# The last six d_ff blocks of a down projection as Strassen-Winograd periods, with two weight sums made by adding transfers

## The reference

```python
h = x + 0.5 * swiglu(rmsnorm(x, g_ffn1), w1g, w1u, w1d)      # FFN 1
u = rmsnorm(h, g_mix)
...                                                          # projections, rotary, two kinds of attention
h = h + concat([oa, ob]) @ w_out
h = h + 0.5 * swiglu(rmsnorm(h, g_ffn2), w2g, w2u, w2d)      # FFN 2
y = rmsnorm(h, final_norm)

def swiglu(x, wg, wu, wd):
    return (jax.nn.silu(x @ wg) * (x @ wu)) @ wd
```

## Time and profile before

| | us |
|---|---|
| median of 3 runs (1061.0 to 1065.07) | 1061.13 |
| the profiled execution's own time | 1062.71 |
| its span, first to last instruction | 1060.9 |
| TensorE busy in the span | 1039.9 (98%) |
| VectorE busy | 835.1 (79%) |
| ScalarE busy | 539.8 (51%) |
| GpSimd busy | 86.7 (8%) |
| mean granted TensorE clock | 0.994 of full speed |

### The profile page before, as it was taken

One profiled execution on the slowest core, in us unless ns is written; L12 is line 12 of the kernel. 1 busy time (PEld: TensorE's weight loads), 2 busy tenths in 40 slices (PEclk: granted clock), 3 DMA queues, 4 the chain that ended last, 5 costly groups with the idle time before them and its releaser, 6 DMA issues. The chain is left out here.

```text
span 1060.9 us, 19168 instructions
## 1 busy us (share of the span) xinstructions
PE 1039.9 (98%) x7698; PEld 1008.7 (95%) x7698; DVE 835.1 (79%) x1257; ACT 539.8 (51%) x929; POOL 86.7 (8%) x84
## 2 busy tenths in 40 slices
PE   9999999999999999988999999999999999999996
PEld 9999999999999999977888889999999999999996
DVE  6999988999878463377777766699998899987744
ACT  7536645666455443344344444544664666645532
POOL 0000000000000034022322102200000000000022
PEclk9999999999999999999999999999999999999998
DMA  5222223223231335220112212213222322223122
GB/s 210 82 80 93 107 82 117 81 87 113 80 120 41 100 114 198 69 86 1 51 50 71 75 41 73 87 40 120 106 94 81 116 84 98 102 80 120 60 61 90
DMA packets 22663, 94.45 MB, mean 89 GB/s; under 512 B 2928, under 2 KB 6000, under 8 KB 16048
## 3 DMA queue, kind: packets, MB, share of 16 engines
q1 hardware_dynamic: 22576, 93.23, 25.4%
HBM read 88.24 MB, written 4.98 MB: 88 GB/s over the span
## 5 line engine op out<-in xcount | busy, mean ns | idle before, releaser
L808 PE MATMUL acc<-c_hi,w_lo 128*128 128x288 f32 x952 | 282.0, 296 | 0.0
L808 PE MATMUL acc<-c_hi,w_hi 128*128 128x288 f32 x952 | 281.1, 295 | 0.0
L808 PE MATMUL acc<-c_lo,w_hi 128*128 128x288 f32 x952 | 277.6, 292 | 0.0
L1564 DVE TENSOR_TENSOR w_lo<-raw,w_hi 128x1024 fp32r<-128x1024 f32 (+3 forms) x161 | 176.4, 1096 | 57.0 <-ACT w_hi L1149 54.3
L808 PEld LDWEIGHTS acc<-c_lo,w_hi 128*128 128x128 f32 x952 | 180.8, 190 | 0.0
L808 PEld LDWEIGHTS acc<-c_hi,w_hi 128*128 128x128 f32 x952 | 179.1, 188 | 0.2
L808 PEld LDWEIGHTS acc<-c_hi,w_lo 128*128 128x128 f32 x952 | 178.6, 188 | 0.0
L1149 ACT ACTIVATE w_hi<-raw 128x1024 fp32r<-128x1024 f32 (+3 forms) x161 | 145.5, 904 | 38.3 <-PE acc L943 17.2
L1297 ACT ACTIVATE comb<-acc 128x288 f32<-128x288 f32 x200 | 82.4, 412 | 151.4 <-PE acc L808 147.4
L1564 DVE TENSOR_TENSOR w_lo<-comb,w_hi 128x1024 fp32r<-128x1024 f32 x100 | 122.1, 1221 | 43.7 <-ACT w_hi L1167 43.7
L808 PE MATMUL acc<-h_hi,w_lo 128*128 128x288 f32 x448 | 132.7, 296 | 0.0
(11 more groups left out here) (222 smaller groups left out, 1699.8 us busy)
## 6 DMA issues: line engine op xcount, KB each, us to landing
raw<-in_w1st SPq DMA_DIRECT2D x17, 1024.0 KB, 4.8
raw<-in_w2st SPq DMA_DIRECT2D x17, 1024.0 KB, 4.8
raw<-in_w1sd SPq DMA_DIRECT2D x8, 1024.0 KB, 4.8
raw<-in_w2sd SPq DMA_DIRECT2D x8, 1024.0 KB, 4.8
raw<-in_w_qk SPq DMA_DIRECT2D x13, 512.0 KB, 3.5
raw<-in_w1gu SPq DMA_DIRECT2D x10, 512.0 KB, 4.6
raw<-in_w2gu SPq DMA_DIRECT2D x10, 512.0 KB, 3.7
raw<-in_w_out SPq DMA_DIRECT2D x8, 512.0 KB, 4.5
```

The lines of the kernel that those rows point to most:

```text
L808: m = nc.tensor.matmul(acc[:, banks[side_of(p)], 0:HALF], w_part[:, col:col + P], x_part, start=n in (P1, P5, P2) and k == 0 and e == 0, s ...
L1564: return nc.vector.tensor_tensor(cols, src, hi.bitcast(FP32), ALU.subtract).then_inc(split_ready, 1)
```

## The change

In each FFN, the plain down projection of d_ff blocks 16 to 21 (8 output blocks, 288 matmuls) is replaced. Six of the output blocks are made by three new periods ("sd", 2, e) of seven block products with 3 inner tiles each (63 matmuls a period), and two output blocks (6 and 7) stay plain (36 matmuls each, `down_block`, PSUM banks 3 and 7, one per token half). Output block 6 stands ahead of the first new period, which is called `BRIDGE`; output block 7 stands behind the last one. So an FFN has 28 periods. The d_ff blocks 17, 19, 21 now get the data combinations of a pair too.

Two of a period's weight sums are no longer made on DVE. The host lays five blocks per period in HBM (the fifth repeats one). SP loads the first three (768 KB in a wide period) as before, and a further two (512 KB, `load_parts`) into the place of the sums. When these have landed, POOL issues a transfer which adds the first two blocks, read from HBM again, to them (`add_weights`, 512 KB, `accum_op`). DVE makes the other two sums by one addition of 512 columns each. `add_weights` is in POOL's queue ahead of `sums`.

The order of the split changes: a1 (P1, P2) first, then the two loaded sums (P5, P7), then the two others (P6, P3), then a22. In the DVE period `hidden` now stands ahead of `weight_sums`, which waits for the adding transfer (`raw_sum`), and the split of the loaded sums stands ahead of `take_c22`, `take_c1` and `add_first`. The residual work of the next norm moves from the loop over `down_block` into the new periods (`FINISHED`): in FFN 1, ACT makes the high part of output block 6 (`next_hi`) ahead of the snap of P1 in `BRIDGE`, and those of blocks 0 and 1, 2 and 3 in the two periods behind it; both FFNs square them there. The first projection of the attention takes its input tiles in the order 6, 0 to 5, 7.

```diff
-RAW_SMALL, RAW_BIG = 1536, 2048
+RAW_SMALL, RAW_BIG = 1280, 1536
-PERIODS += [("st", f) for f in range(TAIL_FROM + 1, KF)]
+PERIODS += [("st", f) for f in range(TAIL_FROM + 1, KF)] + [("sd", 2, e) for e in range(KH - 1)]
+BRIDGE = PERIOD_AT[("sd", 2, 0)]
+ORDER = [KD - 2] + list(range(KD - 2)) + [KD - 1]
+FINISHED = {BRIDGE: (0,), BRIDGE + 1: (1, 2), BRIDGE + 2: (3, 4)}
...
@@ SP @@
+            def load_parts(ffn, p):
+                slot = LANDING[period_key(ffn, p)][0] - RAW_SLOTS
+                n = width(p)
+                sp.dma_start(loaded_sums[slot][:, 0:2 * n], period_weights(ffn, p)[:, 3 * n:5 * n]).then_inc(parts_in[slot], 16)
...
-                    load_block(period_key(ffn, p), src, 4 * PART)
-                for d in range(KD):
-                    load_block(("dn", ffn, d), a[("w1d", "w2d")[ffn]][d], TAIL * P)
+                    load_block(period_key(ffn, p), period_weights(ffn, p)[:, 0:3 * width(p)], 3 * width(p))
+                    if p == 1:
+                        sp.wait_ge(c_ready, KH * (ffn + 1))
+                    if p:
+                        load_parts(ffn, p)
...
@@ TensorE @@
                 for p in range(N_PERIODS):
+                    if p == BRIDGE:
+                        down_block(ffn_no, KD - 2)
                     period_products(ffn_no, p)
-                for steps in (range(TAIL - 1), range(TAIL - 1, TAIL)):
-                    down_block(ffn_no, 0, steps)
-                    down_block(ffn_no, 1, steps)
-                for d in range(2, KD - (1 if ffn_no else 0)):
-                    down_block(ffn_no, d)
...
@@ ScalarE: period(ffn_no, p), wait_finished @@
                 wait_snaps_free(ffn_no, p)
+                if done and ffn_no == 0:
+                    next_hi(ffn_no, done[0])
                 snap(snap_g[:, p % 2, 0, :], ffn_no, p, P1)
+                if done[1:] and ffn_no == 0:
+                    next_hi(ffn_no, done[1])
                 snap(snap_u[:, 1, :], ffn_no, p, P5)
+                if done:
+                    next_square(ffn_no, done[0])
                 snap(snap_g[:, p % 2, 1, :], ffn_no, p, P6)
...
+                if p == BRIDGE - 1:
+                    pair_hi_e(ffn_no, KF - 2)
+                    hi_down(ffn_no, KD - 2, 0)
+                    snap(snap_u[:, 0, :], ffn_no, p, P7)
+                    hi_down(ffn_no, KD - 2, 1)
+                    hi_a1(ffn_no, p + 1)
+                    silu(ffn_no, KF - 1)
+                    take_c21(ffn_no, p)
+                    pair_hi_b(ffn_no, KF - 1)
+                    hi_loaded_sums(ffn_no, p + 1)
+                    pair_hi_a(ffn_no, KF - 1)
+                    hi_sums(ffn_no, p + 1)
+                    return
+            def wait_finished(ffn_no, i):
+                d = ORDER[i]
+                if d >= KD - 2:
+                    act.wait_ge(res_ready, DOWNS_BEFORE[ffn_no] + d - (KD - 2) + 1)
...
@@ VectorE: weight_sums, period(ffn_no, p) @@
-                nc.vector.tensor_tensor(w_sum[:, 0:4:2, :], blocks[:, 0:2, :], blocks[:, 1:3, :],
-                                        ALU.add).then_inc(sum_ready, 1)
+                dve.wait_ge(raw_sum[slot - RAW_SLOTS], count)
+                nc.vector.tensor_tensor(w_sum[:, 0, 0:n], loaded[:, 0, :], blocks[:, 1, :], ALU.add).then_inc(sum_ready, 1)
...
                 lo_a22(ffn_no, p)
-                if f is None:
+                if p == BRIDGE:
+                    down_out(ffn_no, KD - 2)
+                elif f is None:
                     add_second(ffn_no, p - 1)
+                if f is not None:
+                    hidden(ffn_no, f)
                 if not last:
                     weight_sums(ffn_no, p + 1)
+                if ffn_no == 0:
+                    for i in FINISHED.get(p, ()):
+                        next_u(1, i)
...
                 if not last:
                     lo_a1(ffn_no, p + 1)
+                    lo_loaded_sums(ffn_no, p + 1)
...
                 else:
                     add_first(ffn_no, p)
                 if not last:
-                    lo_sums(ffn_no, p + 1, 1)
+                    lo_sums(ffn_no, p + 1)
...
@@ GpSimd @@
+            def add_weights(ffn):
+                for p in range(N_PERIODS):
+                    key = period_key(ffn, p)
+                    slot, count = LANDING[key]
+                    gp.wait_ge(parts_in[slot - RAW_SLOTS], count)
+                    n = 2 * width(p)
+                    nc.gpsimd.dma_start(loaded_sums[slot - RAW_SLOTS][:, 0:n], period_weights(ffn, p)[:, 0:n],
+                                        accum_op=ALU.add).then_inc(raw_sum[slot - RAW_SLOTS], 16)
+            add_weights(0)
             sums(1)
```

More of the change, by code:

```diff
@@ L99, in make_counts @@
     at = [0, 0, 0]
-    run, landed = [None, 0], [0] * (RAW_SLOTS + BIG_SLOTS)
+    run, landed = [None, 0, []], [0] * (RAW_SLOTS + BIG_SLOTS)
     def place(key, n_groups, n_units):
[L103 to L112, removed]
+        kind = {"st": "big", "sd": "big", "dn": "dn"}.get(key[0], "small")
+        if kind == "dn":
+            room[key] = split_after[loads[("dn", key[1], KD - 2) if key[2] == KD - 1 else ("st", key[1], PLAIN)]]
+        else:
+            if run[0] != kind:
+                run[:] = [kind, at[0] - 1, []]
+            n_slots = BIG_SLOTS if kind == "big" else RAW_SLOTS
+            slot = len(run[2]) % n_slots + (RAW_SLOTS if kind == "big" else 0)
+            former = run[2][-n_slots] if len(run[2]) >= n_slots else run[1]
+            landed[slot] += 16
+            landing[key] = slot, landed[slot]
+            room[key] = split_after[former] if former >= 0 else 0
+            run[2].append(at[0])
         loads[key], groups[key], units[key] = at
@@ L835, in ffn, with down_block @@
+            def down_block(ffn, d):
+                for k in range(TAIL):
+                    wait_down(ffn, d, k)
+                    m = down_products(ffn, d, k)
+                m.then_inc(block_used, 1)
             def ffn(ffn_no):
@@ L1322, in period @@
                 former = PERIODS[p - 1] if p else ("st", PLAIN - 1)
[L1323 removed]
+                f = former[1] if former[0] == "st" and p != BRIDGE else None
+                done = FINISHED.get(p, ())
                 if p == 0:
[L1325 removed]
+                    hi_sums(ffn_no, p)
                 elif f is not None:
@@ L1347, in period @@
                     hi_a1(ffn_no, p + 1)
+                else:
+                    hi_down(ffn_no, KD - 1, 0)
+                    hi_down(ffn_no, KD - 1, 1)
                 snap(snap_u[:, 0, :], ffn_no, p, P7)
-                if f is not None and f % 2 and f < TAIL_FROM:
+                if not last:
+                    hi_loaded_sums(ffn_no, p + 1)
+                if f is not None and f % 2:
                     pair_hi_a(ffn_no, f)
                 if not last:
-                    hi_sums(ffn_no, p + 1, 1)
-                else:
-                    hi_block(("dn", ffn_no, 1))
-                    take_c21(ffn_no, p)
-                    silu(ffn_no, KF - 1)
-                    hidden_hi(ffn_no, KF - 1)
+                    hi_sums(ffn_no, p + 1)
+                elif ffn_no == 0:
+                    hi_block(("qk", 0))
             def residual_next(norm, d, count):
@@ L1774, in plain_gate_up @@
                     weight_sums(ffn_no, 0)
-                    lo_sums(ffn_no, 0, 0)
                     lo_a1(ffn_no, 0)
+                    lo_loaded_sums(ffn_no, 0)
                     gate_out(ffn_no, f)
@@ L1856, in period @@
                     lo_a1(ffn_no, p + 1)
+                    lo_loaded_sums(ffn_no, p + 1)
+                else:
+                    lo_down(ffn_no, KD - 1, 0)
+                    lo_down(ffn_no, KD - 1, 1)
                 if f in (PAIRED - 1, TAIL_FROM - 1):
```

466 lines of the change are left out of this document (275 added, 191 removed).

## The result

The changed kernel takes 1071.32 us (median of 4 executions, 1070.95 to 1074.42) against 1063.06 beside it (1061.0 to 1065.07): the ratio is 1.0081, 95% interval 1.0064 to 1.0098. It is slower by 8.3 us. Forecast were 1058 us and most likely no difference; the range, 1053 to 1072, holds the time, but by luck: its top was set by an adding transfer that lands late, which didn't happen, and the sign of the change is the other one. The profiled execution has a span of 1068.7 against 1060.9 us.

A forecast was written before the change was run, and what follows sets the result against it. TensorE, with no idle time worth speaking of, bounds the kernel. 7.6 us gained less stalls of 3.65, 0.55 and 0.2 leaves 3.2: profiled 1062.71 becomes 1059.5, or 1058 us from the median 1061.13; range 1053 to 1072.

The forecast's parts named there:

- a rival of 0.10 at 3 us: Short periods: GpSimd's five additions of squares and VectorE hinder each other, by half hidden, 3 us more (1061); chance 0.10.
- the predicted stalls: FFN 1's bridge: TensorE waits 1.9 us at P6, then 0.8 and 0.95 in the next two periods, together 3.65 us.
- At the ends nothing is lost: Ends of both FFNs: splits, squares and POOL's additions finish before they are needed, so no time is lost.
- the margin that was called thin: End of FFN 2: last POOL addition ends 3.5 us after the last period, final sums stand at 4.0.
- "0.2" for the `st` to `sd` places: Where the first `sd` periods follow: `pair_lo_a` ends within 0.2 us of its need; 0.05 us each in four places.
- the 4.4 of stalls predicted: Stalls subtracted from the gain: 3.65 us in FFN 1's bridge, 0.55 in FFN 2's, 0.2 at the `st` to `sd` places.
- FFN 2's bridge: Short periods of FFN 2: `lo_sums` behind `add_first` is late, 0.25 us at P6 and 0.3 in the period behind.
- the gain of 54 matmuls (7.6 us): Down projection of both FFNs: 27 matmuls and 3.80 us less per FFN, 7.6 us for both.
- VectorE's 1.2 us a period: Wide periods: one sum fewer gives VectorE 1.2 us back each; alone this moves nothing, TensorE being full.
- 5.5 us predicted: Adding transfer in wide periods: takes 5.5 us, 4.8 as for 1024 KB plus 0.7 for POOL's issue, at no cost.
- The limit of 9.2 us: Loop over two periods, 13.0 + L against 22.2: adding transfer L costs nothing up to 9.2 us, hidden by 3.7.
- the rival of the late transfer: `weight_sums` in every period: adding transfer over 9.2 us makes VectorE wait, 25 us per microsecond; chance 0.21.

## Why the prediction was wrong

**The step that failed is GpSimd beside VectorE.** It stood as a rival of 0.10 at 3 us, "five additions of squares ... by half hidden", while the sum took 0.87 and 0.9 us for the splits of the short periods, their length with nothing beside them. They took 1.71 and 1.91. The price was in the earlier trace rows and belonged in the sum, since the change itself moves these additions from the down projection, where VectorE had time, into periods in which it has none. Without the additions the predicted stalls come out almost as worked out: 2.10, 0.95 and 0.95 measured, 1.9, 0.8 and 0.95 predicted (all at P6; the 0.25 us expected at P7 in the later two didn't come). The additions make them 2.10, 1.70 and 1.88. With the ends and the tail they cost 5.9 us by the medians; 1.4 us of stall in this is GpSimd's own time ahead of the final sums, not its hold on VectorE. The rule of the Trainium skill quoted in the prediction ("SBUF — State Buffer", Who interferes with whom) agrees with these runs, and the stretch is larger than in that row: an operation of 0.45 us took up to 1.70.

**"At the ends nothing is lost"** failed twice. In FFN 1 the projection block's load has its room from the split of the last down block, and was not followed at all: 2.7 us by the run with the earlier room. In FFN 2 the margin that was called thin was negative: 1.4 us ahead of the final sums. The tail behind them was 1.6 longer in the profiled execution, but 15.1 us, as before, in another run's with the same wait (the sums on VectorE), so that part is not the change's for certain.

**"0.2" for the `st` to `sd` places** was 2.4. The five combinations stand behind the split of the loaded sums on both engines and end at 122.5 for a tile due at 122.2; they were taken as ending within 0.2 us. Shown by the run that exchanges them.

Put together: the median of before was 1063.1 in this comparison, less 7.6, plus the 4.4 of stalls predicted, 1059.9. To it come 5.9 for GpSimd, 2.2 for the four places, and 0.5 of the 2.7 at the end of FFN 1 (its other 2.2 are gone without GpSimd's additions too), 1068.5. Of the 2.8 us left 0.6 are FFN 2's bridge (below). The other 2.2 no run measured by themselves: the traces show 1.6 us of small waits, and falls of the clock behind the stalls, at 1.6 us each, come and go between executions.

**Right:** the gain of 54 matmuls (7.6 us); VectorE's 1.2 us a period (9.14 became 8.00); the mechanism and place of the stall in FFN 1's bridge; and the adding transfer, 5.5 us predicted, 5.7 in the median, without cost to TensorE. That size was partly luck, since no row stood behind its 0.7 us for POOL's issue (it is 0.87, within the 5.7) nor behind the adding itself. **The limit of 9.2 us** was wrong without effect: the loads take 5.8 us in the mean and 6.1 to the issue of the adding transfer, not 5.6, and the loop has waits that a sum of VectorE's durations leaves out. By the two runs with a longer transfer it lies between 6.3 and 7.2, so the margin was 0.6 to 1.5 us and not 3.7, and the rival of the late transfer was far nearer than it looked.

**FFN 2's bridge**, 0.55 predicted, had 1.13 and 0.56; 0.57 of the first are GpSimd's (0.56 without it). The rest, 0.6 us, is the order of `add_first` ahead of `lo_sums`, as named, but larger.

## What to carry to other kernels

When work moves into a stretch where an engine has no room, every operation that comes with it there, on other engines too, is to be priced beside that engine: a row of the contention in the trace of before belongs in the sum and is not a rival. Moving single operations out of a full engine's way pays only if they don't land beside the same neighbour; the early additions gained nothing alone. At the end of a stage follow each wait of the first instruction behind it (block, load, room for the load), not only the last arithmetic.

## What the runs showed of the hardware

- An adding transfer of 512 KB from HBM into SBUF takes 5.2 to 6.6 us from issue to landing in the changed kernel (8.1 and 8.8 for the first of each FFN) and 0.85 to 0.89 us of GpSimd to issue; one of 8 KB takes 2.3 in one buffer and mostly 3.7 to 5.0 in the other.
- VectorE operations with two inputs from SBUF beside a GpSimd addition of 576 columns (1.4 to 1.5 us alone): 0.45 became 1.70, 0.75 became 1.99, 0.94 became 1.91, 0.96 became 1.71. The extra, 0.75 to 1.25 us, is at most the GpSimd operation's length, and the shortest VectorE operation got as much as the longer ones.
- The granted clock of TensorE falls towards its lower level behind a stall, but not behind each. In all five traces with 0.79 us of waiting at 22 us it was 0.57 to 0.62 at 24 to 28 us; in the nine others, with 0.61 or less, it stayed at 1.00. Behind the 2.1 us in FFN 1's bridge it fell in three traces (0.62 to 0.78 in four microseconds) and stayed at 1.00 in three. Such a fall cost about 1.6 us (15 matmuls, 0.107 us more each), and the spread of the executions goes with the mean clock.
